# Another order for the steps of two layer norms, and for the compression tiles, in a three-layer fp32 block

## The reference, cut to what matters

```
for layer in range(2):
    y = mixer[layer](x)                  # ends in a product with w_out, 2048 x 2048
    x = layernorm(ALPHA * x + y, ln_w[layer], ln_b[layer])
# layernorm: mean and variance over the 2048 features of a token,
#            (x - mu) * rsqrt(var + 1e-6) * w + b
# layer 1 opens with x @ ml_w_in, its first 2048 columns go through a causal
# convolution of width 4 and silu; the third block opens with rms_norm(x) @ w_in_2,
# and a part of its output, in windows of 32 tokens, goes through cmp_w1 (2 x 32
# matrices of 64 x 64), gelu and cmp_w2 (the "compression")
```

## Time and profile before

| | |
|---|---|
| time, median of 3 | 2117.18 us (2116.6 to 2118.67) |
| the profiled execution | 2115.51 us |
| its span in the profile | 2114.0 us |
| PE busy | 2045.6 us, 97% |
| DVE busy | 1394.2 us, 66% |
| ACT busy | 1040.2 us, 49% |
| HBM read | 352.41 MB, 168 GB/s over the span |

### The profile page before, as it was taken

The page is one execution under the profiler, slowest core; times in us unless marked ns, Lnnn a source line. Parts: engine busy times, 40 slices in busy tenths (PEclk is TensorE's granted clock), DMA queues, the critical chain, the costliest instruction groups (busy, mean ns, idle before and its releaser), DMA issues.

```text
span 2114.0 us, 29174 instructions
## 1 busy us (share of the span) xinstructions
PE 2045.6 (97%) x11592; PEld 1759.7 (83%) x11592; DVE 1394.2 (66%) x2154; ACT 1040.2 (49%) x1644; POOL 0.2 (0%) x4
## 2 busy tenths in 40 slices
PE   9999999989999999998999888999999999999999
PEld 7888878868787888887888777888888888888888
DVE  6656667796457676878657876766666556666654
ACT  5545444564445654455365544554444334444432
POOL 0000000000000000000000000000000000000000
PEclk9999999999999999999999999999999999999999
DMA  7453324435542355443654222555555455555553
GB/s 287 184 191 140 120 80 180 157 135 186 181 158 107 133 200 190 173 155 122 234 185 155 100 100 100 201 194 183 195 184 198 181 196 183 189 190 188 191 203 116
DMA packets 52807, 356.41 MB, mean 169 GB/s; under 512 B 5776, under 2 KB 9112, under 8 KB 10432
## 3 DMA queue, kind: packets, MB, share of 16 engines
q1 hardware_dynamic: 49872, 351.04, 45.6%
q10 hardware_dynamic: 2800, 3.50, 0.5%
HBM read 352.41 MB, written 2.11 MB: 168 GB/s over the span
## 4 chain that ended last, share of the span: by engine, by line
PE 79%; DVE 14%; ACT 5%; issue 2%; DMA 1%; SPq 0%; ACTq 0%; DVEq 0%
PE bank L998 78%; DVE WL L1861 5%; ACT WH L1395 2%; DMA X<-in_x 1%; DVE AR L2029 1%; DVE AR L2169 1%; ACT X L1544 1%; DVE AR L2013 0%; DMA raw<-in_W 0%; DVE AR L2047 0%; DVE AR L1878 0%; ACT XP L1543 0%; DVE AR L2228 0%; DVE AR L2046 0%; DVE AR L2137 0%
## 5 line engine op out<-in xcount | busy, mean ns | idle before, releaser
L1861 DVE TENSOR_TENSOR WL<-raw,WH 128x1024 fp32r<-128x1024 f32 x653 | 790.9, 1222 | 374.3 <-ACT WH L1395 364.2
L1395 ACT ACTIVATE WH<-raw 128x1024 fp32r<-128x1024 f32 x653 | 683.8, 1055 | 473.5 <-PE bank L998 419.3
L998 PE MATMUL bank<-XP,WH 128*128 128x512 f32 (+2 forms) x2224 | 722.3, 399 | 25.0 <-DVE WL L1861 17.1
L998 PEld LDWEIGHTS bank<-XP,WL 128*128 128x128 f32 (+1 forms) x2144 | 408.5, 191 | 89.4 <-DVE WL L1861 1.7
L998 PE MATMUL bank<-FP,WH 128*128 128x512 f32 x1408 | 443.3, 396 | 0.6 <-DVE X L1873 0.6
L998 PE MATMUL bank<-XP,WL 128*128 128x256 f32 (+2 forms) x2144 | 440.0, 281 | 1.2 <-DVE WL L1861 1.2
L998 PEld LDWEIGHTS bank<-XP,WH 128*128 128x128 f32 (+1 forms) x2224 | 355.0, 191 | 44.1 <-issue 19.3
L998 PEld LDWEIGHTS bank<-FP,WL 128*128 128x128 f32 x1408 | 264.5, 188 | 62.2
L998 PE MATMUL bank<-FP,WL 128*128 128x256 f32 x1408 | 277.3, 278 | 0.0
L998 PE MATMUL bank<-AP,WH 128*128 128x512 f32 x704 | 222.0, 395 | 0.0
L998 PEld LDWEIGHTS bank<-FP,WH 128*128 128x128 f32 x1408 | 214.8, 189 | 1.3 <-DVE X L1873 0.9
(11 more groups left out here) (301 smaller groups left out, 1645.4 us busy)
## 6 DMA issues: line engine op xcount, KB each, us to landing
raw<-in_W SPq DMA_DIRECT2D x330, 1024.0 KB, 4.8
out<-AR ACTq DMA_DIRECT2D x16, 128.0 KB, 2.0
X<-in_x SPq DMA_DIRECT2D x3, 512.0 KB, 10.4
raw<-in_W SPq DMA_DIRECT2D x2, 512.0 KB, 5.9
AR<-rv SPq DMA_DIRECT2D x1, 1024.0 KB, 8.0
cst<-in_cst ACTq DMA_DIRECT2D x1, 963.0 KB, 12.9
X<-in_x SPq DMA_DIRECT2D x2, 256.0 KB, 3.9
AR<-in_sgu SPq DMA_DIRECT2D x1, 512.0 KB, 5.7
```

The source lines that it names most:

```text
L998: return pe.matmul(o, lhsT, rhs, start=start, stop=stop)
L1395: ac.activation(w_slot(WH, s), raw_half(hf), ACT.Copy).then_inc(s_hi, 1)
L1861: tt(w_slot(WL, s), raw_half(pl.half_of[s]), w_slot(WH, s).bitcast(F32), ALU.subtract).then_inc(s_lo, 1)
```

## The change

What moves:

- In `proj`, an output step is put before the block of its tile is closed, and one at a time: with groups (4, 4) in `conv` the outputs 0 and 1 stand at T947 and T955, and 2 to 9 at T963, 967, 971, 975, 979, 983, 987 and 995. The second group of `conv` has four blocks instead of three, with bank 5 among its banks.
- The fold of the sums (six additions) leaves `res_out(15)` for a step of its own at the tenth tile of the last block of `wo0` and `wo1` (T825, T1929).
- `norm`: counted in pieces of four tiles from the start of `conv` or `p1`, the table load stands at 1, ln sums at 4, ln stats at 5, the root and the low parts 12 to 15 at 6, and ln chunk 0 to 9 at 8, 10, 12, 14, 17, 19, 21, 24, 26 and 28.
- At ln chunk j VectorE works on chunk j and on the low part of chunk j-2, ScalarE on chunk j-1. Before: j, j-1 and j.
- rs square 0 and 1 stand at chunks 8 and 9, rs square 2 behind `p1`.
- The compression tiles of block b stand behind the tiles of block b+1 of `d`; the weights are packed in that order.

```diff
@@ -60,7 +60,7 @@
-    t_blocks("ml_w_in", [r(128 * b, 128) for b in range(16)], DM, (AHEAD, 3))
+    t_blocks("ml_w_in", [r(128 * b, 128) for b in range(16)], DM, (AHEAD, 4))
     t_blocks("ml_w_in", [r(6144, 8) * 4 + r(6152, 8)], DM)
@@ -74,10 +74,12 @@
     d0 = c0 + 1024
-    for b in range(8):
-        t_blocks("w_in_2", [r(d0 + 128 * b, 128)], DM)
-        for l in range(8 * b, 8 * b + 8):
-            tiles.append(("cmp_w1_2", l // 32, [l % 32], "bd"))
+    for b in range(9):
+        if b < 8:
+            t_blocks("w_in_2", [r(d0 + 128 * b, 128)], DM)
+        if b > 0:
+            for l in range(8 * b - 8, 8 * b):
+                tiles.append(("cmp_w1_2", l // 32, [l % 32], "bd"))
     for b in range(4):
@@ -196,10 +198,12 @@
-    def __init__(self, name, n, nk, by, ko=0, width=0, kb=(3, 5, 6, 7), pair=True, half=True, ahead=0):
+    def __init__(self, name, n, nk, by, ko=0, width=0, kb=(3, 5, 6, 7), pair=True, half=True, ahead=0,
+                 norm=None):
         self.name, self.n, self.nk, self.by, self.width, self.kb = name, n, nk, by, width, kb
         self.groups = ko if isinstance(ko, tuple) else (ko,)
-        self.ko, self.ahead = sum(self.groups), ahead
+        self.ko, self.ahead, self.norm = sum(self.groups), ahead, norm
         self.pair = pair and not width
@@ -300,11 +304,13 @@
-        due, first, ends = [], [], list(itertools.accumulate(st.groups))
+        due, ends = [], list(itertools.accumulate(st.groups))
         for n, k in tile_order(st.n, st.nk, st.groups):
             if k == 0:
                 self.bank_of[st.name, n, 0] = st.kb[n] if n < st.ko else self.next_bank()
             i = self.tile(st, n, k)
+            if due and (n >= st.ko and k % 4 == 3 or n == st.ko - 1 and n >= st.ahead > 0 and k in (12, 14)):
+                self.out(st, due.pop(0))
             if k == st.nk - 1:
@@ -312,18 +318,15 @@
                 elif n + 1 in ends:
-                    first += range(n + 1 - st.groups[ends.index(n + 1)], n + 1)
+                    due += range(n + 1 - st.groups[ends.index(n + 1)], n + 1)
+                while n == st.n - 1 and due:
+                    self.out(st, due.pop(0))
             elif n == st.ahead - 1 and k % 2:
                 self.closes.add(i)
-            if first and (n >= st.ko and k % 4 == 3 or n == st.ko - 1 and n >= st.ahead > 0 and k in (12, 14)):
-                self.out(st, first.pop(0))
-            if due and (due[0] < n and k == 3 or n == st.n - 1 and k == st.nk - 1):
-                while due:
-                    self.out(st, due.pop(0))
+            if st.norm is not None and n == st.n - 1 and k == 9:
+                self.say("ln fold", st.norm)
             if n + 1 in ends if by_k and n < st.ko else len(self.of_tile) % 4 == 0 if n < st.ko else k % 4 == 3:
                 yield
-        while first:
-            self.out(st, first.pop(0))
@@ -386,10 +389,10 @@
            *(Stage(f"kn{g}", 4, 4, "dve", pair=False) for g in range(4)), *(Stage(f"v{g}", 1, 4, "act", 0, 512) for g in range(4)),
-           Stage("wo0", 16, 16, "dve", 3, 0, (0, 1, 2), half=False), Stage("conv", 16, 16, "dve", (AHEAD, 3), 0, (0, 1, 2, 4, 3, 6, 7), ahead=AHEAD),
+           Stage("wo0", 16, 16, "dve", 3, 0, (0, 1, 2), half=False, norm=0), Stage("conv", 16, 16, "dve", (AHEAD, 4), 0, (0, 1, 2, 4, 3, 5, 6, 7), ahead=AHEAD),
            Stage("gates", 1, 16, "dve", pair=False),
            Stage("vm", 4, 16, "act", 0, 512), Stage("o", 16, 16, "dve"), Stage("mz", 16, 16, "dve"),
-           Stage("wo1", 16, 16, "dve", KO, half=False), Stage("p1", 8, 16, "dve", (AHEAD, 4), 0, (0, 1, 2, 4, 3, 5, 6, 7), ahead=AHEAD),
+           Stage("wo1", 16, 16, "dve", KO, half=False, norm=1), Stage("p1", 8, 16, "dve", (AHEAD, 4), 0, (0, 1, 2, 4, 3, 5, 6, 7), ahead=AHEAD),
            Stage("vsw", 1, 16, "dve", 0, 280),
@@ -474,19 +477,19 @@
-    def norm(layer, g, fifths):
-
-
-        go(g, 3)
-        say("ln sums", layer)
-        say("ln stats", layer)
-        at = 3
-        for j in range(9):
-            go(g, (30 + fifths * j) // 5 - at)
-            at = (30 + fifths * j) // 5
-            say("ln chunk", j)
-            if layer and j in (4, 6, 8):
-                say("rs square", j // 2 - 2)
+    def norm(layer, g):
+
+
+        steps = {1: ["ln table"], 4: ["ln sums"], 5: ["ln stats"], 6: ["ln root", "ln low"]}
+        for at in range(29):
+            for name in steps.get(at, ()):
+                say(name, layer)
+            j = (10 * at - 80 + 22) // 23
+            if at >= 8 and (80 + 23 * j) // 10 == at:
+                say("ln chunk", j)
+                if layer and j >= 8:
+                    say("rs square", j - 8)
+            go(g, 1)
@@ -495,7 +498,7 @@
     cv = p.proj(st["conv"])
-    norm(0, cv, 12)
+    norm(0, cv)
     go(cv)
@@ -532,11 +535,12 @@
     p1 = p.proj(st["p1"])
-    norm(1, p1, 14)
+    norm(1, p1)
     go(p1)
     p.big, p.turn = [0, 1, 2, 4], 0
     vs = p.proj_tm(st["vsw"], out=False)
     say("hot in")
+    say("rs square", 2)
     say("rs add", 1)
@@ -549,13 +553,14 @@
         g = p.proj(st["d"])
-        for b in range(8):
-            for _ in range(4):
+        for b in range(9):
+            for _ in range(4 if b < 8 else 0):
                 next(g)
                 yield
-            for l in range(8 * b, 8 * b + 8):
-                i = p.tile("cmp", l // 32, l % 32, "cmp tile")
-            p.closes.add(i)
+            if b > 0:
+                for l in range(8 * b - 8, 8 * b):
+                    i = p.tile("cmp", l // 32, l % 32, "cmp tile")
+                p.closes.add(i)
         go(g)
@@ -1526,13 +1531,12 @@
                 W = ln_parts(layer)
-                exp_table()
                 ac.wait_ge(s_lvar, layer + 1)
                 rstd(W["rs"], W["dd"], 1, 0).then_inc(s_lrs, 1)
             def ln_chunk(layer, g):
-                if g == 8:
+                if not 0 <= g < 8:
                     return
@@ -1568,10 +1572,12 @@
                     hi(n)
-                elif what == "ln stats":
+                elif what == "ln table":
+                    exp_table()
+                elif what == "ln root":
                     ln_root(0)
                 elif what == "ln chunk":
-                    ln_chunk(0, n)
+                    ln_chunk(0, n - 1)
                 elif what == "conv out":
@@ -1675,10 +1681,12 @@
                     (offset_part if n < AHEAD else second_half)("p1", n, blk(RAW, n))
-                elif what == "ln stats":
+                elif what == "ln table":
+                    exp_table()
+                elif what == "ln root":
                     ln_root(1)
                 elif what == "ln chunk":
-                    ln_chunk(1, n)
+                    ln_chunk(1, n - 1)
                 elif what == "rs square":
@@ -2020,28 +2028,29 @@
+            def add(to, what):
+                chain(tt(to, to, what, ALU.add))
+
+            def ln_fold(layer):
+
+                W, i6 = ln_parts(layer), 6 * layer
+                D, B, S, Q = W["D"], W["B"], W["S"], W["Q"]
+                dv.wait_ge(s_lsh, i6 + 4)
+                add(S, blk(D, 12, 2))
+                dv.wait_ge(s_lsq, i6 + 4)
+                add(Q, B[:, 0:512])
+                for t in (S, Q):
+                    add(t[:, 0:T], t[:, T:2 * T])
+                dv.wait_ge(s_lsh, i6 + 5)
+                add(S[:, 0:T], blk(D, 14))
+                dv.wait_ge(s_lsq, i6 + 5)
+                add(Q[:, 0:T], B[:, 512:768])
+
             def res_out(layer, n):
                 name, W, i6 = f"wo{layer}", ln_parts(layer), 6 * layer
                 D, A, B, S, Q = W["D"], W["A"], W["B"], W["S"], W["Q"]
-                def add(to, what):
-                    return chain(tt(to, to, what, ALU.add))
-
-                def fold(t):
-                    return tt(t[:, 0:T], t[:, 0:T], t[:, T:2 * T], ALU.add)
-
-                if n == 15:
-                    dv.wait_ge(s_lsh, i6 + 4)
-                    add(S, blk(D, 12, 2))
-                    chain(fold(S))
-                    dv.wait_ge(s_lsq, i6 + 4)
-                    add(Q, B[:, 0:512])
-                    chain(fold(Q))
-                    dv.wait_ge(s_lsh, i6 + 5)
-                    add(S[:, 0:T], blk(D, 14))
-                    dv.wait_ge(s_lsq, i6 + 5)
-                    add(Q[:, 0:T], B[:, 512:768])
                 dv.wait_ge(*done(name, n))
@@ -2101,7 +2110,6 @@
                     tt(Q[:, 0:T], Q[:, 0:T], B[:, 768:1024], ALU.add).then_inc(s_lq, 1)
-                    ln_low_ahead(layer, 12, 13, 14, 15)
@@ -2135,8 +2143,8 @@
                     tt(d, d, to_all(W["mrs"], 2), ALU.add).then_inc(s_lsc, 1)
-                if g > 0:
-                    ln_low(layer, g - 1)
+                if g > 1:
+                    ln_low(layer, g - 2)
@@ -2151,12 +2159,16 @@
                     res_out(0, n)
+                elif what == "ln fold":
+                    ln_fold(0)
             for what, n in pl.steps["conv"]:
```

(6 more changed lines are left out.)

## The result

The changed kernel takes 2097.72 us (median of 4, 2093.93 to 2103.36) against 2117.93 (median of 4, 2116.6 to 2118.93) for the kernel before, measured side by side: ratio 0.9907, 95% interval 0.9879 to 0.9935 (a ratio is not exactly the quotient of the two medians). It is faster, by 20.2 us where 23.5 were forecast. The profiled execution is the longest of its four, 2103.36 us with a span of 2101.9. The page: the same work, in less idle time.

A forecast was written before the change was run, and what follows sets the result against it. The prediction took ScalarE and VectorE waiting for each other to hold back PE behind both layer norms. Its terms, -11 - 13 + 0.5 = -23.5 us, gave a median of 2093.7 us, range 2086 to 2106.

The forecast's parts named there:

- What bounds the stages: Behind both layer norms: ScalarE and VectorE wait for each other in a circle, 5.65 us a turn against PE's 2.81.
- VectorE's sum already sets both stages: Rival for both norm stages: the order of work does not matter, no gain, 2117 us; chance 0.04.
- half of it: Rival: coupling costs 0.5 us more a turn, 17 turns in each layer; -8 to -18, about 2103 us; chance 0.18.
- Layer 0: Term for the first norm stage, up to T1016 in `conv`: taken as -11 us, from -7 to -13.
- the walk: Following three engines through the new list: -11.9 us in layer 0, -15.0 in layer 1; chance 0.62 for 2089 to 2099.
- Layer 1: Term for the second norm stage, from T1936 to T2084: taken as -13 us, from -8 to -15.
- The 2 us charged for the clock behind the new stop: In layer 1: the new 1.7 us stop lowers PE's clock, charged at 2 us; none charged in layer 0.
- The new stops: At T840 and T1944: PE stops 1 to 2 us there, and its stop ahead of the sums is gone.
- The fourth block: In the second group of `conv`: gives PE 8 tiles a pair of low parts in place of 6; no separate price.
- The compression tiles: Term for `d`: the 2.25 us stop goes, but PE waits for lo 296; +0.5 us, from -3 to +3.
- one stop of 3.8 us ahead of lo 296: In `d`: PE reaches T2109 at 1000.1 and waits 3.8 us, the clock falling behind it as behind the old stop.
- slower: Rival: short waits keep PE at 1.2 GHz in both norm stages, +77 against -23.5, at worst 2171 us; chance 0.04.

The follow-up runs named there:

- fold_back: The changed kernel with the six additions of the fold back at the head of block 15's work; 2097.10 us, ratio 0.9892 to the kernel before.
- conv_three: The changed kernel with three blocks instead of four in the second group of `conv`; 2097.61 us, ratio 0.9890 to the kernel before.
- cmp_only: The kernel before with only the compression tiles put a block later; 2122.31 us, ratio 1.0010 to the kernel before.
- cmp_back: The changed kernel with the compression tiles of block b behind block b again; 2091.97 us, ratio 0.9853 to the kernel before.
- pool_late: The changed kernel with lo 296 ahead of a memset and the gates, and two memsets moved to GpSimd; 2092.11 us, ratio 0.9855 to the kernel before.

## Why the prediction was right, and where a size was off

- **What bounds the stages** was right. The circle of ScalarE and VectorE was the cause: opening it alone gives 15.4 us in the two layers, closing it in the kernel after takes back 20.6 of 26.7 (10.8 and 9.8). The rival that VectorE's sum already sets both stages falls with this, and so does "half of it": the turn is 3.07 us, the very sum of VectorE's three pieces, with no 0.5 us for coupling.
- **Layer 0**: the walk gave -11.9, I took -11; T1016 comes 12.3 us earlier as counted from T832 (391.92 to 469.19, before 89.5 us), the stretch is 12.16 shorter. PE's last stop is at T1016, as worked out. The bounds of -7 and -13 were not needed.
- **Layer 1**: the walk gave -15.0, I took -13 and measured -14.52. The 2 us charged for the clock behind the new stop were not there: the stop is 1.50 us (1.7 forecast), matmuls behind its like in layer 0 are not slow (the pair at 396.47 took 0.51 us where the pair behind the old stop took 0.99), and the clock of the stretch is 1.00. By the Trainium skill, page "TensorE: Matmul & The Clock Gate", section "A second HAM failure mode: psum-queue depth-cycling", frequent short idle spells between groups of matmuls make the clock fall and rise again and again. The stops of this stretch (1.50, 0.90 and 0.87 us and two of 0.2) did not do so (clock 1.00); the two close together in `d` did come ahead of such a fall. In `vsw` PE has stops of 0.90 and 0.87 us; I had worked out about 3 us of waiting.
- **The new stops**: 1.50 us at T840 and at T1944 instead of 3.35 and 3.36, as forecast. fold_back puts the whole of the fold at 3.0 us.
- **The fourth block** is worth 2.3 us by conv_three; I had put it into the walk without a price of its own, and my expectation for conv_three gave it less and for a reason that did not hold (VectorE's work, where PE's own from T984 on sets the end).
- **The compression tiles: the mis-sized term.** I took +0.5 us, from -3 to +3, with one stop of 3.8 us ahead of lo 296 and "the clock falls behind this stop as it did behind the old one". The runs show +1.3 to +5.5 us against the kernel before, 3.6 in the mean, just outside the term's own bounds. The stops were smaller than forecast (1.48 and 1.29) and the low clock behind them larger than behind the old one: that clause of the step is what failed. The step also overlooked the end of the stage, where the last two groups of compression tiles come together and the clock falls once more in six of nine executions.
- **Luck in the sum.** With the walks as measured and the mean for `d`, -12.2 - 14.5 + 3.6 is -23.1, beside the -23.5 forecast: layers 0 and 1 gained 2.7 us more than taken, `d` lost 3.1 more. The first measurement, -20.2, and the second, -25.3, lie on either side.
- **The clock as a rival** ("slower") had its chance from stages of short stops. It did not come about in the stages of the norms. It did come in `d`, at 5 us in the first profile and not at 77; I had allowed 3 at most for `d`.

What stays open: why the clock is lower for longer in one execution than in another of the same kernel, in both places of `d` (0.95 over 103.75 us, 0.92 over 105.62) and behind the stop at 182 us, and whether setting the last two groups of compression tiles apart would win back the second loss of `d`. No run explains the one or tries the other.

## What to carry to other kernels

When two in-order engines alternate on the same item and one of them also feeds a third stream (here `hi`, then lo), look for idle time on both in the same turn; staggering one of them by an item turned the sum of their latencies into the larger of their busy times here (5.65 to 3.07 us), and only then did earlier starts and a bigger group pay in full. If a stop comes from a block of work on another engine, moving a consumer past it moves the stop; count what the block holds, and take work out of it. When a consumer is put one block later, look at the end of the stage too, where the last two of its groups fall together. And judge a part of a few microseconds by a stretch cut at the same instructions in both traces, since the granted clock elsewhere moves the whole time by as much.

## What the runs showed of the hardware that was not expected

- The same stop had different consequences. PE waits 1.73 us for ScalarE near 182 us. Timeline of PE, kernel before:

```profile
182.40 0.50 PE L998 MATMUL bank<-CP,WH 128*128 128x256 f32 x2 [1.73 <-ACT AR L1473]
```

Kernel after:

```profile
182.05 0.50 PE L1003 MATMUL bank<-CP,WH 128*128 128x256 f32 x2 [1.73 <-ACT AR L1478]
```

Behind it the clock stays at 1.00 in the one and falls to the lower level, 1.2 GHz, in the other (mean 0.58 from 183 to 195 us), with the same instructions. cmp_only, which does not differ from the kernel before up to there, has it too, and cmp_back, which is the kernel after up to there, has not. It costs 4.1 us at this place (lo 64 starts at 201.99 instead of 197.91).
- Executions of one kernel differ by 5 to 14 us. 23 of the kernel before on one chip went from 2115.8 to 2128.6, at mean clocks of 0.988 and 0.983. Over the span 0.005 is some 10 us, so by this estimate the clock can account for most of it.
- GpSimd's memset of 128 x 2048 floats took 1.82 and 1.81 us, VectorE's 1.76, and VectorE's lo beside the second took 1.20 (1.22 otherwise). Timeline of GpSimd, pool_late:

```profile
896.66 1.82 POOL L2603 MEMSET AR<- 128x2048 f32 x1 [896.22 <-PE bank L1005]
970.32 1.81 POOL L2605 MEMSET AR<- 128x2048 f32 x1 [71.84 <-DVE AR L2321]
```
